# Two gate tiles computed by seven products instead of eight, gates kept in SBUF, weight sums added earlier

## What is computed

```python
proj = h @ w_in[l]
(q_a, k_a, v_a, z_a, q_b, k_b, v_b, z_b,
 f_logit, g_logit) = jnp.split(proj, split_points, axis=-1)
y_a = _from_heads(_stick_breaking(...q_a, k_a, v_a...))
y_a = (y_a * jax.nn.silu(z_a)) @ w_o_sb[l]
...
y_b = _from_heads(_forgetting_attention(...q_b, k_b, v_b..., cum_log_f))
y_b = (y_b * jax.nn.silu(z_b)) @ w_o_fox[l]
gates = jax.nn.sigmoid(g_logit + b_gate[l]).reshape(b, s, N_BRANCH, d)
merged = gates[:, :, 0, :] * y_a + gates[:, :, 1, :] * y_b
x = x + gate[:, None, :] * (merged @ w_out[l])
```

## Time and profile before

| what | value |
|---|---|
| median of 3 runs | 1241.84 us (1241.63 to 1242.46) |
| the profiled execution | 1239.95 us, its span 1238.1 us |
| granted TensorE clock | 1.00, the upper of its two levels |
| TensorE busy | 1212.9 us of the span |
| VectorE, ScalarE, GpSimd busy | 855.8, 654.1, 430.3 us |

### The profile page before, as it was taken

How to read it: one execution, slowest core, us unless ns; L and a number is a source line. 1 busy time by engine, 2 the same in 40 slices (tenths; PEclk the granted TensorE clock), 3 DMA queues, 4 the chain that set the end, 5 groups by cost and what they waited for, 6 DMA issues and landing times.

```text
span 1238.1 us, 22894 instructions
## 1 busy us (share of the span) xinstructions
PE 1212.9 (98%) x9270; PEld 1041.4 (84%) x9270; DVE 855.8 (69%) x1342; ACT 654.1 (53%) x1028; POOL 430.3 (35%) x330
## 2 busy tenths in 40 slices
PE   6999999999999999999999989999999999999999
PEld 6798999876767888777787768788878999999999
DVE  4289897789653275696647757356568888878974
ACT  6555463777665533463446544454335555556452
POOL 5562000422333745455343035540555223333000
PEclk9999999999999999999999999999999999999999
DMA  9953332666977974766321018851533555556554
GB/s 387 357 202 128 117 109 97 245 215 219 264 197 169 252 269 168 241 152 151 92 103 37 4 69 308 261 136 29 147 123 100 158 187 186 187 171 211 186 186 142
DMA packets 42182, 215.53 MB, mean 174 GB/s; under 512 B 5080, under 2 KB 5208, under 8 KB 28128
## 3 DMA queue, kind: packets, MB, share of 16 engines
q1 hardware_dynamic: 34272, 140.74, 31.9%
q0 software_dynamic: 4608, 28.31, 12.1%
q10 hardware_dynamic: 3200, 45.04, 9.8%
HBM read 206.72 MB, written 63.98 MB: 219 GB/s over the span
## 4 chain that ended last, share of the span: by engine, by line
PE 85%; DVE 8%; ACT 4%; issue 2%; POOL 1%; DMA 0%; ACTq 0%; SPq 0%; DVEq 0%; POOLq 0%
PE banks L663 83%; PE banks L670 2%; DVE arena L2603 1%; DVE arena L2600 1%; DVE arena L2605 1%; DVE h_low L2344 1%; POOL weights_low L3289 1%; ACT weights_high L1492 0%; ACT arena L1546 0%; POOL arena L3348 0%; DMA arena<-in_mem 0%; DVE arena L2434 0%; DVE weights_low L2344 0%; DVE gact_low L2344 0%; DVE arena L3240 0%
## 5 line engine op out<-in xcount | busy, mean ns | idle before, releaser
L3289 POOL TENSOR_TENSOR weights_low<-weights,weights_high 128x512 fp32r<-128x512 f32 (+1 forms) x216 | 309.7, 1463 | 494.4 <-ACT weights_high L1492 494.4
L663 PE MATMUL banks<-h_high_low,weights_high 128*128 128x512 f32 (+1 forms) x696 | 243.4, 350 | 0.4 <-DVE h_low L2344 0.3
L663 PE MATMUL banks<-h_low,weights_high 128*128 128x512 f32 (+1 forms) x696 | 235.9, 339 | 0.0
L663 PE MATMUL banks<-h_high_low,weights_low 128*128 128x512 f32 (+1 forms) x696 | 235.9, 339 | 0.0
L1492 ACT ACTIVATE weights_high<-weights 128x2048 fp32r<-128x2048 f32 (+2 forms) x86 | 126.9, 1488 | 61.3 <-PE banks L663 58.4
L663 PEld LDWEIGHTS banks<-h_high_low,weights_high 128*128 128x128 f32 x696 | 131.3, 189 | 19.4 <-issue 3.0
L663 PEld LDWEIGHTS banks<-h_low,weights_high 128*128 128x128 f32 x696 | 131.2, 189 | 16.5 <-issue 2.4
L663 PEld LDWEIGHTS banks<-h_high_low,weights_low 128*128 128x128 f32 x696 | 131.2, 188 | 16.0
L663 PE MATMUL banks<-arena 64*64 64x64 f32 (+6 forms) x1800 | 116.7, 263 | 1.9 <-POOL arena L3348 0.7
L663 PEld LDWEIGHTS banks<-arena 64*64 64x64 f32 (+3 forms) x1800 | 85.0, 147 | 24.2 <-issue 17.3
L3367 POOL TENSOR_TENSOR weights_low<-weights,weights_high 128x512 fp32r<-128x512 f32 x32 | 48.5, 1538 | 112.6 <-ACT weights_high L1504 112.6
(11 more groups left out here) (463 smaller groups left out, 3292.4 us busy)
## 6 DMA issues: line engine op xcount, KB each, us to landing
weights<-in_stream SPq DMA_DIRECT2D x66, 1024.0 KB, 5.7
up_sums<-in_up POOLq DMA_DIRECT2D x16, 1024.0 KB, 9.8
weights<-up_sums SPq DMA_DIRECT2D x64, 256.0 KB, 2.9
weights<-in_up SPq DMA_DIRECT2D x48, 256.0 KB, 2.9
sums_kept<-in_down POOLq DMA_DIRECT2D x16, 704.0 KB, 7.0
arena<-in_ada SPq DMA_DIRECT2D x8, 1024.0 KB, 11.9
weights<-sums_kept SPq DMA_DIRECT2D x9, 704.0 KB, 4.2
sums_kept<-in_down ACTq DMA_DIRECT2D x8, 704.0 KB, 6.5
```

The costliest lines, as they stand in the source:

```text
L663: ins = nc.tensor.matmul(o, lhsT, rhs, start=start, stop=stop, skip_group_check=skip)
L3289: nc.gpsimd.tensor_tensor(lo_of(c)[:, cols], raw_of(c)[:, cols], hi_of(c)[:, cols].bitcast(F32), ALU.subtract).then_inc(sem("weights_split ...
```

## The change

- The pair of gate tiles 10 and 11 joins the first projections, as the sixth of now twelve pairs; the stream is laid out anew for it. `EARLY_G`, the number of gate tiles that go the plain way, falls from 12 to 10, so nothing stands between gate tile 9 and the output projections.
- Tiles 10 and 11 are written to where k_b goes later, sent to DRAM two pairs on (0.5 MB), and fetched in step 4 of the forgetting branch to where they stay. VectorE waits for the sending before it writes the first tile of k_b.
- Tiles 12 to 15 go in step 1 of attention from the arena to `sums`, within SBUF (1 MB), instead of to DRAM, and ScalarE reads them from there at the end. Nothing is fetched back behind attention.
- TensorE's wait for the last moves of the first projections stands in step 2 instead of step 1. Gate tiles 8 and 9 take banks 2 and 3 first.
- VectorE makes the low parts of the first four gated tiles within the forgetting branch (steps 5, 9, 13, 17), the other four behind it.
- ScalarE splits the third chunk of the output projections between gates 13 and 14, the fourth behind all gates.
- GpSimd begins the adds behind the chunk `vb + 3`. The numbers of all chunks from v_b on to gate tile 9 are one higher than before.

```diff
-EARLY_TILES = (("qa", 1), ("ka", 0), ("ka", 1), ("za", 0), ("za", 1), ("qb", 0), ("qb", 1), ("kb", 0), ("kb", 1), ("g", 6), ("g", 7))
+EARLY_TILES = (("qa", 1), ("ka", 0), ("ka", 1), ("za", 0), ("za", 1), ("g", 5), ("qb", 0), ("qb", 1),
+               ("kb", 0), ("kb", 1), ("g", 6), ("g", 7))
-Z_FIRST, EARLY_G = EARLY_TILES.index(("za", 0)), 12
+Z_FIRST, EARLY_G = EARLY_TILES.index(("za", 0)), 10
...
-        gates = [at(512 * m if m < EARLY_G else GATES_AT + 512 * (m - EARLY_G), T) for m in range(16)]
+        gates = [at(512 * m if m < 12 else GATES_AT + 512 * (m - 12), T) for m in range(16)]
+        early_gates = {5: at(8192, 2, T), 6: at(GATES_AT, 2, T), 7: at(GATES_AT + 2 * T, 2, T)}
...
-                if i == 1:
+                if i == LAG:
                     pe.wait_ge(sem("product_moved"), MOVED0)
...
-                        M.use([0, 1, 2, 3])
+                        M.use([2, 3, 0, 1])
...
+                    if e >= 2 and EARLY_TILES[e - 2] == ("g", 5):
+                        act.wait_ge(sem("product_moved"), early_moved(e - 2, C12))
+                        act.dma_start(gates_kept, at(8192, 2 * T)).then_inc(sem("keys_kept"), 16)
...
                     act.wait_ge(sem("product_moved"), MOVED0)
-                    act.dma_start(gates_kept, at(GATES_AT, 4 * T)).then_inc(sem("keys_kept"), 16)
+                    act.dma_start(sums.rearrange("p a b -> p (a b)"), at(GATES_AT, 4 * T)).then_inc(sem("keys_kept"), 16)
                 if i == 2:
                     act.wait_ge(sem("nF_stored"), 16)
-                    act.wait_ge(sem("keys_kept"), 48)
+                    act.wait_ge(sem("keys_kept"), 64)
...
+                if i == 4:
+                    act.dma_start(at(512 * EARLY_G, 2 * T), gates_kept).then_inc(sem("keys_kept"), 16)
...
-            act.dma_start(at(GATES_AT, 4 * T), gates_kept).then_inc(sem("keys_kept"), 16)
             for m in range(SIDE_G, EARLY_G):
                 gate_out(m)
                 gate_inverse(m)
-            act.wait_ge(sem("keys_kept"), 64)
+            act.wait_ge(sem("keys_kept"), 80)
             for m in range(EARLY_G, 16):
-                link(nc.scalar.activation(gates[m], gates[m], ACT.Exp, scale=-1.0, bias=npar("b_gate", m)))
+                if m == 14:
+                    split_weights()
+                src = gates[m] if m < 12 else sums[:, m - 12, :]
+                link(nc.scalar.activation(gates[m], src, ACT.Exp, scale=-1.0, bias=npar("b_gate", m)))
                 inverse(gates[m]).then_inc(sem("gates"), 1)
-            for _ in range(2):
-                split_weights()
+            split_weights()
...
                 if f == P2:
+                    if EARLY_TILES[e] == ("kb", 0):
+                        dve.wait_ge(sem("keys_kept"), 48)
...
+            def gated_split(m):
+                dve.wait_ge(sem("gated_hi"), m + 1)
+                low(gated_lo[:, m, :], gated_raw[:, m, :], gated_hi[m], sem("gated_split"))
...
+                if i % 4 == 1 and 5 <= i <= N + 1:
+                    gated_split(i // 4 - 1)
...
-            for m in range(8):
-                dve.wait_ge(sem("gated_hi"), m + 1)
-                low(gated_lo[:, m, :], gated_raw[:, m, :], gated_hi[m], sem("gated_split"))
+            for m in range(4, 8):
+                gated_split(m)
...
-            low_weights(0, vb + 5)
-            for c in range(4):
-                low_weights(vb + 5 + c, vb + 6 + c)
-                add(S1, A22, 2, c)
-                add(S3, A11, 2, c)
-            for c in range(4, 8):
-                low_weights(vb + 5 + c, vb + 6 + c)
+            low_weights(0, vb + 3)
+            for c in range(8):
+                low_weights(vb + 3 + c, vb + 4 + c)
                 add(S1, A22, 2, c)
                 add(S3, A11, 2, c)
-            low_weights(vb + 13, mixers + 1)
+            low_weights(vb + 11, mixers + 1)
```

More of the change, by code:

```diff
@@ L556, in early_tile @@
             if key == "g":
-                return gates[2 * c + half][:, TH * side:TH * (side + 1)]
+                return early_gates[c][:, half, TH * side:TH * (side + 1)]
             to = {"qa": qa, "ka": ka, "za": gated["a"], "qb": qb, "kb": kb}[key]
@@ L3513, in lay_stream @@
         if i == 5:
-            parts.append(by_gates[EARLY_G // 2:])
-    parts.append(by_gates[:EARLY_G // 2])
+            parts.append(by_gates[6:])
+        if i == 3:
+            parts.append(by_gates[5:6])
+    parts.append(by_gates[:5])
     parts.append(lay_chunks(np.asarray(a["w_o_sb"])[0], 512))
@@ L3570 @@
     nF_kept = nc.dram_tensor("nF_kept", [HEADS, T], F32, kind="Internal").ap()
-    gates_kept = nc.dram_tensor("gates_kept", [P, 4 * T], F32, kind="Internal").ap()
+    gates_kept = nc.dram_tensor("gates_kept", [P, 2 * T], F32, kind="Internal").ap()
     sums_kept = nc.dram_tensor("sums_kept", [4, DOWN_PAIRS, P, DOWN_W], F32, kind="Internal").ap()
```

## The result

| | before | after |
|---|---|---|
| median of the runs of one comparison (us) | 1241.74 (1239.26 to 1242.46, 4 runs) | 1253.26 (1252.62 to 1253.89, 4 runs) |
| profiled execution (us) | 1239.95 | 1253.89 |
| its span (us) | 1238.1 | 1252.1 |
| mean granted clock | 1.000 | 0.996 |
| start of attention (us) | 222.13 | 231.93 |

The ratio is 1.0103, 95% interval 1.0085 to 1.012: slower, by 12.8 us by this ratio (the two medians of four runs each lie 11.5 us apart), where 1.3 us less was forecast. The span of the profiled executions grew by 14.0 us. Code lines behind the change have other numbers in the new kernel: the two product lines are L665 and L672, the scans L2613, VectorE's normalisation L2672, GpSimd's split L3305 and its add of up sums L3318.

A forecast was written before the change was run, and what follows sets the result against it. TensorE's issue of products was taken as the bound: 11.25 us removed, 9.96 us added, all other terms 0, so 1.29 us less, the median going from 1241.84 to 1240.55 us; range 1238.7 to 1243.5 us.

The forecast's parts named there:

- The sum: TensorE's products: gate tiles 10 and 11 removed, 11.25 us; one more first-projection pair added, 9.96 us; net 1.29 us less.
- The saving copy: Start of attention: 1 MB copied within SBUF, assumed to take 5.9 us as the DRAM store did, so 0.
- Rival (d): First value tile's eviction: the copy within SBUF lands late; at 11.8 us the kernel takes 1246.3 us; chance 0.09.
- (e): Output projection: second chunk late behind ScalarE, then GpSimd; 3.5 us late gives 1242.8 us, double that 1245 us; chance 0.07.
- Nothing there waited for it: The 1 MB restore, halved and moved from the end into attention: nothing at the end waited for it, so no gain.
- One collision for another: I take 0: Attention: GpSimd's split moves from scans of 256 columns to scans of 384; net 0, bounds -1.05 and +1.7 us.
- rival (c): Attention: GpSimd's adds collide more than before, up to +1.7 us; 1242.2 us, no difference; chance 0.14.
- The end of attention: Output projection starts without tiles 10 and 11 as cover; second chunk has 1.2 us to spare, so 0.
- This pays nothing: End of attention: ScalarE's 3.17 us wait for the sums goes, but TensorE was not waiting there, so no gain.
- Half of the gated tiles are split within attention, where TensorE sets the pace: Attention's steps: VectorE's moved splits of half the gated tiles, taken to cost 0.
- the trade: 48 products of gate tiles 10 and 11 exchanged for 84 of an extra pair: 1.29 us less on TensorE.

The follow-up runs named there:

- e10: As e7, but in each step the split of the gated tile stands behind VectorE's normalisation: 1239.65 us beside 1240.23 us, ratio 1.0002.
- e11: Kernel after, with the fetch of gates 10 and 11 at step 5, directly behind the load of the forget rows: 1245.64 us, ratio 1.004.
- e2: Kernel after, with the fetch of gates 10 and 11 moved from step 4 to step 10, adds still early: 1247.15 us, ratio 1.0053.
- e3: Kernel before, with only GpSimd's adds moved sooner, behind vb+3: 1245.71 us, ratio 1.0045.
- e1: Kernel after, with GpSimd's adds put back behind vb+5: 1255.62 us, ratio 1.0127.
- e6: Kernel after, with the fetch at step 10, adds from vb+4, sixth and seventh adds both behind vb+9: 1241.46 us, ratio 1.0003.
- e7: As e6, with the last four copies of down sums behind the load of the forget rows on ScalarE's queue: 1241.44 us, ratio 1.0003.
- e8: Kernel after, with the fetch at step 10, adds at vb+3, all copies of sums issued two steps sooner: 1241.09 us, ratio 1.0002.
- e4: Kernel after, with GpSimd's adds one chunk later, vb+4 for vb+3: 1249.21 us, ratio 1.0063.

## Why the prediction was wrong, step by step

**The sum** held. A pair costs 9.96 us, and with the waits taken out (e10) the output projection begins 1.50 us sooner, for 1.29 us forecast; the difference is accounted for above.

**The saving copy** held: 4.5 us for an assumed 5.9 us, no wait. Rival (d) did not come, nor (e): no wait for GpSimd's split behind 415 us.

**"Nothing there waited for it"** is the first step that failed. The sentence ("halved, moved into attention and off the end, but nothing there waited for it") asks who waits at the end for the fetch of gates 10 and 11, and so puts its move at nothing. It has no term for the place to which the fetch goes: behind it in ScalarE's queue stands the 0.5 MB load of the forget rows, for which VectorE waited 0.5 us already before. The prediction has no row of it. Measured: the rows landed 8.7 us later by the fetch's place ahead of them (e11), TensorE waited 6.8 us, and with the adds as early as in the kernel after this cost 6.1 us (e2) to 7.6 us (e11) of total time. The sooner adds have a part in it, since they make the same rows 5 us later (e3), and with the fetch alone TensorE waits at most 1.3 us at a time (e1). That term is missing too: the prediction priced the adds only by their collision with a scan, not by their traffic.

**"One collision for another: I take 0"** is the second, and this is rival (c) with its price mis-sized. When the first add is released was right (302.42 us, which less the 9.80 us by which attention is later is 292.6 us, for 293 us forecast), and so was where the split falls (293.9 us in that frame, 294.8 us forecast). The old collision did go: the pair of scans of 256 columns takes 1.27 us, for 1.28 us expected. And the sign named for (c) came, a scan above 2 us and a wait between 270 and 325 us. The price was wrong. Two more collisions of 1.05 us were the upper bound, taken from scans beside one half of a chunk. The split of a whole chunk that has piled up cost VectorE 4.2 us and TensorE 3.5 us. Then comes a term that the sum did not have: 1.6 us lost to a lower clock behind that wait, and 1.5 us behind the other. Rival (c) was priced at 1.7 us; the adds alone cost 5.6 us (e3).

**The end of attention** was judged rightly in its place and wrongly in its size. "This pays nothing" is right for the kernel as changed. But the sooner adds are there for it: left at vb+5 they cost 7.7 us of waits at the end (e1).

**"Half of the gated tiles are split within attention, where TensorE sets the pace"** was 1.6 us off in e6 and e7. These splits stand ahead of a normalisation for which TensorE's transposes wait. In the trace this is about all that the trade saves, and it explains why e6, e7 and e8 came out at the time of before.

By the runs: 5.6 us for the adds (e3) and 6.1 to 7.6 us for the place of the fetch with these adds (e2, e11) are 11.7 to 13.2 us; the splits in the steps and the trade nearly cancel. 12.8 us were measured.

## What to carry to other kernels

When a transfer is moved, ask not only who waits for it but what it is put ahead of in its own queue, and how late that may be; with DMA busy throughout, 0.5 MB ahead cost the next load 8.7 us here. Two delays of one load that are harmless each can make a wait together. When an in-order engine gets a wait, the work that piles up behind it comes in one block, and that block can hit a neighbour that had never met more than half of it. Price a new wait of TensorE of several microseconds with what the clock may take afterwards: in attention it was 1.5 to 2.4 us a wait in four traces (after, e3, e4, e11) and nothing in a fifth (e2).

## What the runs showed of the hardware

- A pair of scans of 384 columns took 1.81 us alone or beside the issue of an add, and 6.01 to 6.26 us beside four splits of GpSimd in a row; in the kernel after all of that is in the first scan, 5.16 us. A split of 512 columns on VectorE took 0.69 us alone, 1.61 us (e6) and 1.76 us (e10) beside GpSimd.
- In attention four traces have a wait of TensorE of 3.5 to 3.7 us. In three of them (after, e3, e11) it was followed by 4 to 5 us below clock 1.00, mostly at 0.50; in e2 the clock stayed at 1.00. Waits of 0.5 us (e6, e7) left the mean clock at 1.000.
- Two loads of 0.5 MB on one queue swapped their landing times (23.3 and 16.8 us against 14.6 and 22.0) when their order was swapped.
- A load of 0.5 MB with nothing else moved on its queue landed in 4.2 us (e7) with GpSimd's queue at rest, and in 11.5 us (e8) with 1.63 MB moved there meanwhile.
- 1 MB from SBUF to SBUF landed in 4.5 us.
